# High and low parts of the activations through one 512-column matmul in the feed-forward stages

## The chip, the cores and the metric

The kernel runs on one NeuronCore of a Trainium2 chip. The metric is the device time of one execution in microseconds, lower is better. All inputs and outputs are float32, and there is one launch.

## The reference

Two transformer-like blocks run one after the other on 256 tokens of width 1024. Between them they hold four SwiGLU feed-forward layers of width 2816 and two squared-ReLU MLPs of width 4096. The other stages are a state-space mixer (S5) and three attentions.

```python
def swiglu(h, w_gate, w_up, w_down):
    return (jax.nn.silu(h @ w_gate) * (h @ w_up)) @ w_down

def first_block(x, ...):                       # DEPTH = 2, D_MODEL = 1024, D_FF = 2816
    h = x                                      # (1, 256, 1024) float32
    for layer in range(DEPTH):
        h = h + 0.5 * swiglu(rms_norm(h, ffn_norm[layer, 0]), ...)
        hn = rms_norm(h, mix_norm[layer])
        h = h + (s5_mixer(hn, ...) if layer % 2 == 0 else moba_mixer(hn, ...))
        h = h + 0.5 * swiglu(rms_norm(h, ffn_norm[layer, 1]), ...)
    return h

def second_block(x, ...):                      # D_FF_2 = 4096
    h = x
    for layer in range(DEPTH):
        hn = rms_norm_2(h, norm_mix_g[layer])
        h = h + (ab attention if layer % 2 == 0 else mla attention)
        hn = rms_norm_2(h, norm_mlp_g[layer])
        h = h + jnp.square(jax.nn.relu(hn @ mlp_w1[layer])) @ mlp_w2[layer]
    return rms_norm_2(h, final_norm_g)
```

## The kernel before, in words

Activations lie feature-major: partition = feature within a block of 128, free axis = the 256 tokens (T). There are KT = 8 such blocks of the width 1024. Every projection in float32 is done in three parts. A matrix W is split as whi = W rounded to the matmul's reduced format (fp32r) and wlo = W - whi, the activations likewise into xhi and xlo, and W x is taken as whi xhi + whi xlo + wlo xhi. One call of `mm3` (L551) issues these three matmuls of 256 columns each, in this order, all into the same half of a PSUM bank; each matmul instruction loads its own stationary 128x128 tile, so whi is loaded twice.

The weights of all stages are one stream of 246 chunks of 128x2048 floats (1 MB). For each chunk n SyncE loads `raw` (three slots), ScalarE casts it into `whi` (`split_hi`, L979; it waits until TensorE has used the chunk three before, semaphore `w_used`), VectorE subtracts to get `wlo` (`split_lo`, L1285), and TensorE waits for `wlo_ready` and runs 48 matmuls on it. A chunk of a gate or up matrix gives 2 x 128 output features (16 `mm3`), a chunk of a down matrix takes 2 x 128 hidden features to all 1024 outputs (16 `mm3`).

The stages ffn0, ffn1, ffn2, ffn3 have 11 iterations of three chunks (gate, up, down), the stages mlp0 and mlp1 16 iterations of two (up, down). The first gate and up of a stage are done ahead by `proj_first` and `proj`, then a loop on every engine runs the rest: `ffn` and `mlp` on TensorE issue for iteration i the gate and up of i and then the down of i-1. `down` adds into banks 0 to 3 over the whole stage. Gate and up go to banks 4 to 7, two pairs in turn in `ffn`, three banks in turn in `mlp`, one bank for each chunk.

VectorE's order within an iteration with first chunk c is: `split_lo(c+2)`, `gate`, `split_lo(c+3)`, `hidden`, `split_lo(c+4)`. `gate` (L1322) reads the bank, multiplies by the inverse root `rstd` of the norm and writes `gs`; ScalarE takes the SiLU of it. `hidden` reads the up bank times rstd into `us` (L1331), multiplies by `gs` (L1336, in the MLPs the squared ReLU, L1338), ScalarE casts to `hhi` (L1018), VectorE subtracts to get `hlo` (L1341), and only then comes `split_lo(c+4)`. All waits are semaphores, and each engine runs its list in the written order. GpSimd prepares tables for the S5 stage while ffn0 runs (L448 to L484).

The sums over the 1024 features for the norm go through bank 7 (`stats`), and ScalarE takes the root from there (`root_ready`).

Of the kernel before, what the change touches and what calls it, by code (L numbers as in the profile page):

```python
# [14 lines left out]
ALU = mybir.AluOpType  # L15
# [33 lines left out]


BEFORE = {}
_it = _swiglu = _n = 0
for _name, _ in STAGES:
    if _name[:3] in ("ffn", "mlp"):
        BEFORE[_name] = dict(gs=_swiglu, us=_it, act=_it, hid=_it, hhi=_it, hlo=_it, acc=3 * _n)
        _its = FFN_IT if _name[:3] == "ffn" else MLP_IT
        _it, _swiglu, _n = _it + _its, _swiglu + (_its if _name[:3] == "ffn" else 0), _n + 1
N_NORMS = len(STAGES) + 1


# [11 lines left out]
def build(nc, wstream, xT, params, tgain, s5b, s5c, causal, onehot, logn, relb, out, scratch):  # L72
# [3 lines left out]
    def S(name):  # L76
        if name not in sems:
            sems[name] = ctx.enter_context(nc.semaphore(name))
        return sems[name]
# [11 lines left out]
    with ctx:  # L91
# [2 lines left out]
        wlo = sb("wlo", [P, NSLOT, CH], F32R)  # L94
        h = sb("h", [P, KT, T])
        at[0] += 448
        xhi = sb("xhi", [P, KT, T], F32R)
        xlo = sb("xlo", [P, KT, T], F32R)
        gs = sb("gs", [P, 2, T])
        us = sb("us", [P, 2, T])  # L100
        at[0] += 32
# [103 lines left out]

        def both(v):
            return v.unsqueeze(1).to_broadcast([P, 2, T])

        def half_bank(b, m):
            return ps[:, b, m * T:(m + 1) * T]  # L210
# [99 lines left out]
        def roots_upto(k):  # L310

            return sum(not token_major(n) for n in range(k + 1))
# [234 lines left out]
        def _(pe):  # L547
# [12 lines left out]
            def proj(n, i, bank, operand=None, wait_k=None, first_k=0, stop_k=None):  # L560
# [12 lines left out]
                if stop_k is None:  # L573
                    last.then_inc(S("w_used"), 1)

            def proj_first(n, bank, wait_k, operand=None):

                ohi, olo = operand or (xhi, xlo)
                slot = n % NSLOT
                chunk_ready(n, None)  # L580
                for k in range(KT):
                    pe.wait_ge(*wait_k(k))
                    for m in range(2):
                        w = slice(m * P, (m + 1) * P)
                        last = mm3(half_bank(bank, m), whi_b[slot][:, k, w], wlo_b[slot][:, k, w],
                                   ohi[:, k, :], olo[:, k, :], k == 0 and m == 0, k == KT - 1)
                last.then_inc(S("w_used"), 1)
# [57 lines left out]
            def ffn(st):  # L645
                F, k = FIRST[st], NORM_OF[st]
                proj_first(F, 4, x_wait(k))
                start_stage(k)
                zero_acc()
                proj(F + 1, None, 5)  # L650
                stats(k)
                with pe.Fori(0, (FFN_IT - 1) // 2) as i:
                    for u in range(2):
                        b, n = (1 + u) % 2, F + 2 + 3 * u

                        proj(n, i, 4 + 2 * b)
                        if u == 0:
                            pe.wait_ge(S("root_ready"), roots_upto(k))
                        proj(n + 1, i, 5 + 2 * b)
                        down(st, n + 2, u, i, u)  # L660
                down(st, F + 3 * FFN_IT - 1, FFN_IT - 1, None, (FFN_IT - 1) % 2, final=True)

            def mlp(st):
                F, k = FIRST[st], NORM_OF[st]
                proj_first(F, 4, x_wait(k))
                stats(k)
                start_stage(k)
                zero_acc()
                with pe.Fori(0, (MLP_IT - 1) // 3) as i:
                    for u in range(3):  # L670
                        n = F + 1 + 2 * u
                        proj(n, i, 4 + (1 + u) % 3)
                        down(st, n + 1, u, i, u)
                down(st, F + 2 * MLP_IT - 1, MLP_IT - 1, None, (MLP_IT - 1) % 3, final=True)

# [596 lines left out]
        def _(dve):  # L1272
# [41 lines left out]
                dve.reciprocal(rstd[:, :], rstd[:, :]).then_inc(S("rstd_ready"), 1)  # L1314
                dve.wait_ge(S("rstd_ready"), n)

            def gate(st, i0, i, b, n_gate):

                dve.wait_ge(S("w_used"), at_iter(n_gate + 1, BODY, i))
                if i0 > 0:  # L1320
                    dve.wait_ge(S("hidden_ready"), at_iter(BEFORE[st]["hid"] + i0, 2, i))
                dve.tensor_tensor(gs[:, :, :], bank2(4 + 2 * b), both(rstd[:, :]), ALU.mult)\  # L1322
                    .then_inc(S("gate_scaled"), 1)

            def hidden(st, i0, i, b, per, n_up):

# [1 line left out]
                swiglu = st.startswith("ffn")  # L1328
                if i0 > 0:
                    dve.wait_ge(S("hidden_lo_ready"), at_iter(BEFORE[st]["hlo"] + i0, per, i))  # L1330
                dve.tensor_tensor(us[:, :, :], bank2(5 + 2 * b if swiglu else 4 + b), both(rstd[:, :]), ALU.mult)\  # L1331
                    .then_inc(S("up_scaled"), 1)
                dve.wait_ge(S("up_scaled"), at_iter(BEFORE[st]["us"] + i0 + 1, per, i))
                if swiglu:
                    dve.wait_ge(S("gate_activated"), at_iter(BEFORE[st]["gs"] + i0 + 1, per, i))
# [11 lines left out]
            def ffn(st):  # L1347
                F, k = FIRST[st], NORM_OF[st]
                split_lo(F + 2)
                inverse_root(k)  # L1350
                gate(st, 0, None, 0, F)
                split_lo(F + 3)
                hidden(st, 0, None, 0, 2, F + 1)
                with dve.Fori(0, (FFN_IT - 1) // 2) as i:
                    for u in range(2):
                        c = F + 2 + 3 * u
                        split_lo(c + 2, i)
                        gate(st, 1 + u, i, (1 + u) % 2, c)
                        split_lo(c + 3, i)
                        hidden(st, 1 + u, i, (1 + u) % 2, 2, c + 1)  # L1360
                        split_lo(c + 4, i)
# [377 lines left out]
```

## Time and profile before

| | |
|---|---|
| median of three runs | 1686.85 us (1685.65 to 1688.14) |
| the profiled execution, its own time | 1688.04 us |
| its span, first to last instruction | 1686.2 us |
| TensorE busy with matmuls | 1600.0 us, 95% |
| VectorE busy | 1088.6 us, 65% |
| ScalarE busy | 760.5 us, 45% |
| GpSimd busy | 465.0 us, 28% |
| mean granted TensorE clock | 0.967 of full |

Busy time of TensorE is the time in which any matmul is in flight; one of 256 columns takes 280 ns from start to end, but the next starts after 113 to 118 ns. So the step from start to start, and not the duration, says what a matmul costs in a dense stretch. Starts in the rows are rounded to 10 ns; a step is therefore read over many matmuls.

### The profile page before, as it was taken

The page shows a single profiled execution, that of the slowest core. Times are in us where ns is not written, and L with a number is a line of the kernel's source. Part 1 is how long each engine was busy: PE and PEld are TensorE (multiplying, and loading weights), DVE is VectorE, ACT ScalarE, POOL GpSimd, SP SyncE. Part 2 cuts the span into 40 slices and gives each one's busy share as a digit, 9 for nine tenths or more (in the row PEclk, how much of TensorE's full clock was granted, in tenths as well). Part 3 has the DMA queues.
Part 4 walks back from the last instruction along what each step waited for, and adds up shares of the span by engine and source line. Part 5 has one row for each costly group of instructions (what it writes and reads, how often), then busy time and mean ns, then how long its engine had stood idle before and what let it go on. Part 6 is the DMA issues. An engine that isn't in the chain of part 4 may idle for free.

```text
span 1686.2 us, 31471 instructions
## 1 busy us (share of the span) xinstructions
PE 1600.0 (95%) x13068; PEld 1531.7 (91%) x13068; DVE 1088.6 (65%) x1067; ACT 760.5 (45%) x995; POOL 465.0 (28%) x413
## 2 busy tenths in 40 slices
PE   5989998799999999999999999999999998999997
PEld 5979997599999999999889999976999996699997
DVE  7798769966555665566566555635655665476565
ACT  5434450055344444347554344655434355654432
POOL 6999517700000100007530000564100023510000
PEclk9989996799999999999999999989999997999999
DMA  6535540045555565554425555340555542045552
GB/s 223 196 129 195 211 151 1 1 154 184 187 199 174 173 218 192 181 199 151 150 103 184 197 191 196 136 182 1 182 192 179 194 175 76 25 171 199 179 198 75
DMA packets 39012, 265.74 MB, mean 158 GB/s; under 512 B 4352, under 2 KB 6400, under 8 KB 7328
## 3 DMA queue, kind: packets, MB, share of 16 engines
q1 hardware_dynamic: 37808, 261.41, 44.6%
q0 software_dynamic: 1136, 3.38, 0.8%
q8 instruction: 49, 0.80, 0.2%
q14 instruction: 19, 0.16, 0.0%
HBM read 263.70 MB, written 1.06 MB: 157 GB/s over the span
## 4 chain that ended last, share of the span: by engine, by line
PE 80%; DVE 10%; POOL 4%; issue 3%; ACT 2%; DMA 0%; DVEq 0%; SPq 0%; POOLq 0%; ACTq 0%
PE ps L549 74%; DVE gst L1465 3%; PE ps L839 2%; PE ps L829 2%; DVE wlo L1285 1%; PE ps L817 1%; DVE xlo L1291 1%; POOL tsq L284 1%; DVE h L1301 1%; DVE t L1439 1%; DVE t L1440 1%; ACT pm L1202 0%; DMA h<-in_xT 0%; POOL pm L413 0%; DVE us L1336 0%
## 5 line engine op out<-in xcount | busy, mean ns | idle before, releaser
L1285 DVE TENSOR_TENSOR wlo<-raw,whi 128x2048 fp32r<-128x2048 f32 x246 | 599.0, 2439 | 250.4 <-ACT whi L979 250.1
L549 PE MATMUL ps<-xhi,whi 128*128 128x256 f32 x2048 | 573.5, 280 | 28.9 <-DVE wlo L1285 16.3
L979 ACT CAST whi<-raw 128x2048 fp32r<-128x2048 f32 x246 | 469.2, 1912 | 252.7 <-PE ps L549 252.6
L549 PE MATMUL ps<-xlo,whi 128*128 128x256 f32 x2048 | 570.2, 278 | 0.0
L549 PE MATMUL ps<-xhi,wlo 128*128 128x256 f32 x2048 | 569.6, 278 | 0.0
L549 PEld LDWEIGHTS ps<-xhi,whi 128*128 128x128 f32 x2048 | 388.1, 189 | 33.8 <-DVE wlo L1285 17.4
L549 PEld LDWEIGHTS ps<-xhi,wlo 128*128 128x128 f32 x2048 | 388.5, 190 | 0.0
L549 PEld LDWEIGHTS ps<-xlo,whi 128*128 128x128 f32 x2048 | 387.5, 189 | 0.1
L549 PE MATMUL ps<-hhi,whi 128*128 128x256 f32 x1216 | 341.8, 281 | 0.2
L549 PE MATMUL ps<-hhi,wlo 128*128 128x256 f32 x1216 | 341.6, 281 | 0.0
L549 PE MATMUL ps<-hlo,whi 128*128 128x256 f32 x1216 | 341.3, 281 | 0.0
L359 POOL TENSOR_TENSOR sq<-sq,power 128x256 f32<-128x256 f32 x10 | 16.6, 1658 | 828.7 <-ACT sq L993 828.7
L549 PEld LDWEIGHTS ps<-hhi,whi 128*128 128x128 f32 x1216 | 228.9, 188 | 0.8 <-issue 0.8
L549 PEld LDWEIGHTS ps<-hlo,whi 128*128 128x128 f32 x1216 | 229.1, 188 | 0.0
L549 PEld LDWEIGHTS ps<-hhi,wlo 128*128 128x128 f32 x1216 | 229.0, 188 | 0.0
L1018 ACT CAST hhi<-us 128x512 fp32r<-128x512 f32 x76 | 47.2, 621 | 346.8 <-DVE us L1336 190.9
L549 PE MATMUL ps<-whi,xhi 128*128 128x256 f32 (+1 forms) x368 | 104.7, 285 | 2.6 <-DVE xlo L1291 2.6
L549 PE MATMUL ps<-whi,xlo 128*128 128x256 f32 (+1 forms) x368 | 102.6, 279 | 0.0
L549 PE MATMUL ps<-wlo,xhi 128*128 128x256 f32 (+1 forms) x368 | 102.5, 279 | 0.0
L1331 DVE TENSOR_TENSOR us<-ps,rstd 128x512 f32<-128x512 f32 x76 | 52.5, 690 | 72.1 <-PE ps L549 72.0
L1341 DVE TENSOR_TENSOR hlo<-us,hhi 128x512 fp32r<-128x512 f32 x76 | 59.2, 779 | 52.9 <-ACT hhi L1018 52.9
L549 PE MATMUL ps<-yhi,whi 128*128 128x256 f32 x256 | 73.4, 287 | 1.3 <-DVE ylo L1557 1.3
(235 smaller groups left out, 2071.3 us busy)
## 6 DMA issues: line engine op xcount, KB each, us to landing
raw<-in_wstream SPq DMA_DIRECT2D x247, 1024.0 KB, 4.9
h<-in_xT SPq DMA_DIRECT2D x1, 1024.0 KB, 7.9
out_hT<-h SPq DMA_DIRECT2D x2, 512.0 KB, 3.0
biasA<-bias_rows POOLq DMA_DIRECT2D x5, 192.0 KB, 5.4
biasB<-bias_rows POOLq DMA_DIRECT2D x3, 192.0 KB, 5.5
braw<-in_s5b POOLq DMA_DIRECT2D x1, 512.0 KB, 3.9
CL<-in_s5c POOLq DMA_DIRECT2D x4, 128.0 KB, 5.1
tg<-in_tgain POOLq DMA_DIRECT2D x1, 384.0 KB, 3.5
```

The lines of the kernel that those rows point to most:

```text
L284: chain(eng.tensor_tensor(m1, x1, s, ALU.mult))
L549: return pe.matmul(o, l, r, start=first, stop=last, skip_group_check=True)
L817: last = pe.transpose(ps[:, 2 + s % 2, kt * T + t * P:kt * T + (t + 1) * P], pm[s % 2][:, t, kt * P:(kt + 1) * P], ident)
L829: last = pe.matmul(o, vtok[:, kt, hd["v"]:hd["v"] + hd["dv"]], pT[s % 2][:, kt, q0:T], start=kt == 0, stop=kt == TT - 1, skip_group_check= ...
L839: last = pe.matmul(ps[:, s % 2, t * T:t * T + w], hd["q"][:, t * P:(t + 1) * P], hd["k"][:, 0:w], start=True, stop=True, skip_group_check= ...
L979: act.copy(whi[:, slot, :], raw[:, slot, :]).then_inc(S("whi_ready"), 1)
L1018: act.copy(hid_hi(b), us[:, :, :]).then_inc(S("hidden_hi_ready"), 1)
L1285: dve.tensor_tensor(wlo[:, slot, :], raw[:, slot, :], whi[:, slot, :], ALU.subtract)\
L1291: dve.scalar_tensor_tensor(out=xlo[:, j, :], in0=h[:, j, :], scalar=gain(k, j), in1=xhi[:, j, :], op0=ALU.mult, op1=ALU.subtract).then_inc ...
L1331: dve.tensor_tensor(us[:, :, :], bank2(5 + 2 * b if swiglu else 4 + b), both(rstd[:, :]), ALU.mult)\
L1341: dve.tensor_tensor(hid_lo(b), us[:, :, :], hid_hi(b), ALU.subtract).then_inc(S("hidden_lo_ready"), 1)
L1465: dve.tensor_tensor_scan(gst[g % 2][:, rr, ri, :], m2, t1[g % 2][:, rr, ri, :], 0.0, ALU.mult, ALU.add).then_inc(S("s5_scan"), 1)
```

## The change

xhi and xlo become the two halves of one tensor `xx`. In the loops of the ffn and mlp stages a new `proj_wide` takes the place of `proj`: for each of the 16 pairs of output block and k, one matmul of 512 columns moves xhi and xlo of that k through whi, into the left and right half of a whole bank, and one of 256 columns adds wlo xhi to the left half. A chunk now fills two banks (one for each block of 128 outputs): gate banks 6 and 7, up banks 4 and 5, the same ones in each iteration. `gate` and `hidden` on VectorE first add the two halves with a `reduce_sum` out of PSUM into `gs` or `us`, and then multiply this by rstd in place. The first gate and up of a stage, the down projections and all other stages stay as they were. In the first pass of the ffn loop the second half of the gate waits for `root_ready` and the second half of the up for the first iteration's `up_scaled`. In the mlp loop each up waits for `up_read`, VectorE's read of the one before.

```diff
-        xhi = sb("xhi", [P, KT, T], F32R)
-        xlo = sb("xlo", [P, KT, T], F32R)
+        xx = sb("xx", [P, 2, KT, T], F32R)
+        xhi, xlo = xx[:, 0], xx[:, 1]
...
+        def parts(b):
+            return ps[:, b:b + 2, :].rearrange("p m (a t) -> p m t a", a=2)
...
+            def proj_wide(n, i, bank, before_second=None):
+                slot = n % NSLOT
+                chunk_ready(n, i)
+                for m in range(2):
+                    if m == 1 and before_second:
+                        pe.wait_ge(*before_second)
+                    w = slice(m * P, (m + 1) * P)
+                    for k in range(KT):
+                        mm(ps[:, bank + m, :].rearrange("p (a t) -> p a t", a=2), whi_b[slot][:, k, w], xx[:, :, k, :],
+                           k == 0, False)
+                        last = mm(half_bank(bank + m, 0), wlo_b[slot][:, k, w], xhi[:, k, :], False, k == KT - 1)
+                last.then_inc(S("w_used"), 1)
...
-                        proj(n, i, 4 + 2 * b)
-                        if u == 0:
-                            pe.wait_ge(S("root_ready"), roots_upto(k))
-                        proj(n + 1, i, 5 + 2 * b)
+                        proj_wide(n, i, 6, before_second=(S("root_ready"), roots_upto(k)) if u == 0 else None)
+                        proj_wide(n + 1, i, 4,
+                                  before_second=(S("up_scaled"), BEFORE[st]["us"] + 1) if u == 0 else None)
                         down(st, n + 2, u, i, u)
...
-                        proj(n, i, 4 + (1 + u) % 3)
+                        pe.wait_ge(S("up_read"), at_iter(BEFORE[st]["wide"] + u, 3, i))
+                        proj_wide(n, i, 4)
                         down(st, n + 1, u, i, u)
...
-                dve.tensor_tensor(gs[:, :, :], bank2(4 + 2 * b), both(rstd[:, :]), ALU.mult)\
-                    .then_inc(S("gate_scaled"), 1)
+                    dve.reduce_sum(gs[:, :, :], parts(6), AX.X).then_inc(S("gate_read"), 1)
+                    dve.wait_ge(S("gate_read"), at_iter(BEFORE[st]["wide"] + i0, 2, i))
+                    src = gs[:, :, :]
+                else:
+                    src = bank2(4)
+                dve.tensor_tensor(gs[:, :, :], src, both(rstd[:, :]), ALU.mult).then_inc(S("gate_scaled"), 1)
...
-                dve.tensor_tensor(us[:, :, :], bank2(5 + 2 * b if swiglu else 4 + b), both(rstd[:, :]), ALU.mult)\
-                    .then_inc(S("up_scaled"), 1)
+                    dve.reduce_sum(us[:, :, :], parts(4), AX.X).then_inc(S("up_read"), 1)
+                    dve.wait_ge(S("up_read"), at_iter(BEFORE[st]["wide"] + i0, per, i))
+                    src = us[:, :, :]
+                else:
+                    src = bank2(5 if swiglu else 6)
+                dve.tensor_tensor(us[:, :, :], src, both(rstd[:, :]), ALU.mult).then_inc(S("up_scaled"), 1)
```

TensorE at the start of the ffn0 loop, before: the gate chunk is triples of 256 columns.

```order
L549 MATMUL ps<-xhi,whi 128x256 [waits wlo_ready]
L549 MATMUL ps<-xlo,whi 128x256
L549 MATMUL ps<-xhi,wlo 128x256
L549 MATMUL ps<-xhi,whi 128x256
L549 MATMUL ps<-xlo,whi 128x256
L549 MATMUL ps<-xhi,wlo 128x256
```

The same place now (`xx` is the tensor that holds xhi and xlo):

```order
L555 MATMUL ps<-xx,whi 128x512 [waits wlo_ready]
L555 MATMUL ps<-xx,wlo 128x256
L555 MATMUL ps<-xx,whi 128x512
L555 MATMUL ps<-xx,wlo 128x256
L555 MATMUL ps<-xx,whi 128x512
L555 MATMUL ps<-xx,wlo 128x256
```

Each triple has become a pair with the same number of columns, one instruction and one load of whi fewer.

VectorE in one iteration of the ffn loop, before (`wlo` is `split_lo`, `gs` the gate, `us` the up and hidden values):

```order
L1285 TENSOR_TENSOR wlo<-raw,whi 128x2048
L1319 REGISTER_ALU
L1321 ISA
L1322 TENSOR_TENSOR gs<-ps,rstd 128x512
L1284 REGISTER_ALU
L1285 TENSOR_TENSOR wlo<-raw,whi 128x2048
L1327 REGISTER_ALU
L1331 TENSOR_TENSOR us<-ps,rstd 128x512
L1333 REGISTER_ALU
L1336 TENSOR_TENSOR us<-us,gs 128x512
L1341 TENSOR_TENSOR hlo<-us,hhi 128x512
```

And now:

```order
L1306 TENSOR_TENSOR wlo<-raw,whi 128x2048
L1340 REGISTER_ALU
L1342 ISA
L1343 TENSOR_REDUCE gs<-ps 128x512
L1348 TENSOR_TENSOR gs<-gs,rstd 128x512
L1305 REGISTER_ALU
L1306 TENSOR_TENSOR wlo<-raw,whi 128x2048
L1352 REGISTER_ALU
L1356 TENSOR_REDUCE us<-ps 128x512
L1361 TENSOR_TENSOR us<-us,rstd 128x512
L1362 REGISTER_ALU
L1365 TENSOR_TENSOR us<-us,gs 128x512
```

A reduction that reads 1024 values in each partition stands ahead of each multiplication by rstd, which now has both operands in SBUF; everything behind it on VectorE, the next `wlo` first, comes later by that.

## Rows read from the trace of the kernel before

**Rows 1.** Page, part 1: busy time and instructions of each engine.

```profile
PE 1600.0 (95%) x13068; PEld 1531.7 (91%) x13068; DVE 1088.6 (65%) x1067; ACT 760.5 (45%) x995; POOL 465.0 (28%) x413
```

**Rows 2.** Chain that ended last, 400 to 570 us: start, length, what.

```profile
407.26 157.06 PE ps L549 x1356
```

**Rows 3.** Groups by form, TensorE: busy us, mean ns; idle before, releaser.

```profile
L549 PE MATMUL ps<-xhi,whi 128*128 128x256 f32 x2048 | 573.5, 280 | 28.9 <-DVE wlo L1285 16.3 <-DVE xlo L1291 12.6
```

**Rows 4.** Windows: length, busy of PE, PEld, DVE, ACT, POOL, clock, DMA.

```profile
81.00:98.00 17.00, 17.00 (x149) 17.00 (x149) 16.17 (x8) 6.90 (x5) 16.68 (x5) 1.00 0.40 131
98.00:116.00 18.00, 10.26 (x89) 10.06 (x87) 17.28 (x5) 6.02 (x4) 17.69 (x5) 0.84 0.30 110
171.00:188.00 17.00, 17.00 (x150) 17.00 (x149) 14.79 (x8) 7.02 (x6) 16.52 (x7) 1.00 0.57 192
430.00:556.00 126.00, 126.00 (x1097) 126.00 (x1096) 73.52 (x53) 51.88 (x38) 0.00 (x0) 1.00 0.56 191
```

**Rows 5.** Timeline of TensorE, an ffn1 projection: first and last of 43 matmuls.

```profile
431.08 0.28 PE L549 MATMUL ps<-xhi,whi 128*128 128x256 f32 x1
...
435.84 0.28 PE L549 MATMUL ps<-xhi,whi 128*128 128x256 f32 x1
```

**Rows 6.** The same, an ffn0 down projection: first and last of 23.

```profile
126.78 0.28 PE L549 MATMUL ps<-hhi,whi 128*128 128x256 f32 x1
...
129.38 0.28 PE L549 MATMUL ps<-hlo,whi 128*128 128x256 f32 x1
```

**Rows 7.** The same, mla stage, 384 columns: first and last of 9.

```profile
1409.06 0.34 PE L549 MATMUL ps<-whi,cqhi 128*128 128x384 f32 x1
...
1410.46 0.34 PE L549 MATMUL ps<-whi,cqlo 128*128 128x384 f32 x1
```

**Rows 8.** The same, 512 columns: first and last of five, twice.

```profile
1413.83 0.40 PE L549 MATMUL ps<-wlo,ckhi 128*128 128x512 f32 x1
...
1414.77 0.39 PE L549 MATMUL ps<-whi,cklo 128*128 128x512 f32 x1
...
1416.10 0.39 PE L549 MATMUL ps<-wlo,ckhi 128*128 128x512 f32 x1
...
1417.03 0.40 PE L549 MATMUL ps<-whi,cklo 128*128 128x512 f32 x1
```

**Rows 9.** Groups by form, VectorE, as Rows 3.

```profile
L1549 DVE TENSOR_REDUCE mx<-ps 128x2 f32<-128x512 f32 x24 | 16.6, 691 | 31.1 <-PE ps L839 31.1
L1547 DVE TENSOR_REDUCE mx<-lg 128x1 f32<-128x128 f32 x8 | 2.3, 287 | 0.3
```

**Rows 10.** Timeline of VectorE in ffn0, 96 to 117 us.

```profile
96.76 5.13 DVE L1285 TENSOR_TENSOR wlo<-raw,whi 128x2048 fp32r<-128x2048 f32 x1
101.81 0.68 DVE L1331 TENSOR_TENSOR us<-ps,rstd 128x512 f32<-128x512 f32 x1
102.53 4.32 DVE L1336 TENSOR_TENSOR us<-us,gs 128x512 f32<-128x512 f32 x1
```

**Rows 11.** Timeline of GpSimd there.

```profile
99.82 6.48 POOL L450 TENSOR_TENSOR Ec<-Ec,etmp 128x2016 f32<-128x2016 f32 x1
106.37 3.97 POOL L451 TENSOR_TENSOR Es<-Es,Ec 128x2016 f32<-128x2016 f32 x1
```

**Rows 12.** Timeline of TensorE there.

```profile
116.58 0.58 PE L549 MATMUL ps<-xhi,whi 128*128 128x256 f32 x1 [8.32 <-DVE wlo L1285]
```

**Rows 13.** Timeline of VectorE, start and first pass of the ffn1 loop.

```profile
400.93 0.68 DVE L1331 TENSOR_TENSOR us<-ps,rstd 128x512 f32<-128x512 f32 x1
...
407.05 0.68 DVE L1322 TENSOR_TENSOR gs<-ps,rstd 128x512 f32<-128x512 f32 x1
409.84 0.69 DVE L1331 TENSOR_TENSOR us<-ps,rstd 128x512 f32<-128x512 f32 x1
410.56 0.69 DVE L1336 TENSOR_TENSOR us<-us,gs 128x512 f32<-128x512 f32 x1
413.75 2.29 DVE L1285 TENSOR_TENSOR wlo<-raw,whi 128x2048 fp32r<-128x2048 f32 x1 [1.12 <-ACT whi L979]
```

More of the change, by code:

```diff
@@ L51 @@
 BEFORE = {}
-_it = _swiglu = _n = 0
+_it = _swiglu = _n = _wide = 0
 for _name, _ in STAGES:
     if _name[:3] in ("ffn", "mlp"):
-        BEFORE[_name] = dict(gs=_swiglu, us=_it, act=_it, hid=_it, hhi=_it, hlo=_it, acc=3 * _n)
+        BEFORE[_name] = dict(gs=_swiglu, us=_it, act=_it, hid=_it, hhi=_it, hlo=_it, acc=3 * _n,
+                             wide=_wide)
         _its = FFN_IT if _name[:3] == "ffn" else MLP_IT
         _it, _swiglu, _n = _it + _its, _swiglu + (_its if _name[:3] == "ffn" else 0), _n + 1
+        _wide += _its - 1
 N_NORMS = len(STAGES) + 1
@@ L653, in ffn @@
                     for u in range(2):
-                        b, n = (1 + u) % 2, F + 2 + 3 * u
-                        proj(n, i, 4 + 2 * b)
-                        if u == 0:
-                            pe.wait_ge(S("root_ready"), roots_upto(k))
-                        proj(n + 1, i, 5 + 2 * b)
+                        n = F + 2 + 3 * u
+                        proj_wide(n, i, 6, before_second=(S("root_ready"), roots_upto(k)) if u == 0 else None)
+                        proj_wide(n + 1, i, 4,
+                                  before_second=(S("up_scaled"), BEFORE[st]["us"] + 1) if u == 0 else None)
                         down(st, n + 2, u, i, u)
@@ L664, in mlp @@
                 F, k = FIRST[st], NORM_OF[st]
-                proj_first(F, 4, x_wait(k))
+                proj_first(F, 6, x_wait(k))
                 stats(k)
@@ L1315, in inverse_root, with gate @@
                 dve.wait_ge(S("rstd_ready"), n)
-            def gate(st, i0, i, b, n_gate):
+            def gate(st, i0, i, n_gate):
                 dve.wait_ge(S("w_used"), at_iter(n_gate + 1, BODY, i))
@@ L1350, in ffn @@
                 inverse_root(k)
-                gate(st, 0, None, 0, F)
+                gate(st, 0, None, F)
                 split_lo(F + 3)
@@ L1357, in ffn @@
                         split_lo(c + 2, i)
-                        gate(st, 1 + u, i, (1 + u) % 2, c)
+                        gate(st, 1 + u, i, c)
                         split_lo(c + 3, i)
```

## The prediction

> **What bounds the kernel now.** I read part 1 of the page first: TensorE has a matmul in flight for 1600 of 1686 us, and its weight loads are busy for 91% [rows 1]. The chain of waits says the same by stage. In ffn1 it is one unbroken piece of 157 us of TensorE from the first down to the end of the stage [rows 2], and the window inside it shows TensorE busy for 126 of 126 us at the full clock (1.00, that is 2.4 GHz) with VectorE at 73.5 of 126, 58% [rows 4]. The same holds for the other ffn and mlp stages. So in those loops two things count: the step from one matmul's start to the next, and whether VectorE's `wlo` keeps coming in time.
>
> The exception is ffn0. GpSimd prepares the S5 tables then. From 98 to 116 us VectorE is busy for 17.28 and GpSimd for 17.69 of 18 us, while TensorE falls to 10.26 and its clock to 0.84 [rows 4], and one wait of 8.32 us for `wlo` ends that stretch [rows 12]. That single wait is half of all that the projections waited for `wlo` (16.3 us) [rows 3]. The reason stands in the timelines. The subtraction that takes 2.29 us when GpSimd is idle [rows 13] takes 5.13 us here; the multiplication us<-us,gs, 0.69 us alone [rows 13], takes 4.32 us; and it ends at 106.85, about 0.5 us after GpSimd's 128x2016 operation ends at 106.30 [rows 10, 11]. GpSimd's operations take 3.97 us, or 6.48 us when VectorE's work falls into them [rows 11]. These two take turns whenever VectorE's operands all lie in SBUF. The multiplications that read PSUM kept their 0.68 us in the very same stretch [rows 10].
>
> **What the change removes on TensorE.** The loops hold 4 x 10 x 2 = 80 gate and up chunks and 2 x 15 = 30 up chunks of the MLPs, 110 in all, with 16 pairs each: 1760 places where two matmuls of 256 columns (and two loads of the same whi) become one of 512. The number of columns stays, so what can be saved is only what a matmul costs beyond its columns.
>
> Now the steps. In an ffn1 projection, 42 steps take 4.76 us, 113.3 ns each [rows 5]; the columns alone are 256 / 2.4 GHz = 106.7 ns, so 6.6 ns lie on top. In a down projection 22 steps take 2.60 us, 118.2 ns [rows 6]. If those 6.6 ns were a fixed price of an instruction, longer matmuls would show them once. They don't. With 384 columns, 8 steps take 1.40 us, 175 ns [rows 7], 15 ns over the 160 of the columns. With 512, 4 steps take 0.94 and 0.93 us, 235 and 232.5 ns [rows 8], 19 to 22 ns over 213.3. The excess grows with the columns: per column 0.443 and 0.462 ns at 256, 0.456 at 384, 0.454 to 0.459 at 512. A matmul of 512 costs as much as two of 256, within the spread of the two kinds of 256.
>
> Two of 256 in these loops are 226.7 ns. For the new one I take 230 ns, between 226.7 and the 232.5 of rows 8, since its moving operand is the one that went at the lower step. That is +3.3 ns x 1760 = +6 us. Bounds from the rows: the bare columns, 213.3 ns, give -13.4 x 1760 = -24 us; the slowest rows, 235 ns for the wide one and 118.2 instead of 113.3 for the narrow one behind it, give (8.3 + 4.9) x 1760 = +23 us.
>
> The Trainium skill, page TensorE: Matmul & The Clock Gate, section Back-to-back issue gap, gives the step as N/2.4 + 2.5 ns, so 216 ns for 512 columns. By it the wide one would save 11 ns a time, about 19 us, and the sum below would be near 1681. The trace does not agree with it at 512 columns of this type (232.5 to 235 ns), so I leave it to a rival.
>
> **What the change adds on VectorE.** Each of the 110 reads gets a reduction over 1024 values in a partition. Reductions of 128 and 512 values take 287 and 691 ns [rows 9], 1.05 ns for each further value, so 1024 take 691 + 539 = 1.23 us. The multiplication behind it now reads SBUF instead of PSUM: 0.69 us without GpSimd, as the 0.69 of PSUM [rows 13]. With the semaphore between them a read costs 1.27 us more.
>
> In ffn1 to ffn3 and both MLPs this is hidden. An ffn iteration is three chunks, 16.6 us, in which VectorE has some 7 us free by the 58%; two conversions take 2.5. The tightest place is the first pass of a loop. TensorE starts the first down at 407.26 [rows 2]; 96 matmuls later, at 118.2 ns, that is at 418.6, it wants the `wlo` that VectorE makes from 413.75 to 416.04 [rows 13]. Both conversions (at 407.05 and 409.84) stand ahead of it, also by way of ScalarE's casts, so it comes at 416.04 + 2.54 = 418.6. It just fits; I take 0, with 1.5 us in all as the upper end. The new waits there are met early: the second half of the loop's first up starts 24 matmuls (2.8 us) before 407.26, at 404.4, and the up before it was read at 400.93 [rows 13], a read that the change leaves as it is. The `up_read` wait of an mlp stage has a whole down projection (48 x 118.2 ns = 5.7 us) to be met in.
>
> In ffn0 nothing hides it. Between 81 us and the end of the long wait at 116.58 VectorE is full (16.17 of 17 and 17.28 of 18 us [rows 4]) and three conversions stand in its list (the us of the iteration before at the start of the stretch, the gs just ahead of the wlo of 96.76, the us of 101.81 [rows 10]). The least that each costs is 1.27 us, 3.8 in all. The most: the multiplication, now with both operands in SBUF, takes a turn behind one more GpSimd operation of 3.97 us [rows 11], so 1.23 + 3.97 = 5.2 each, 15.6 in all. I take 3 each, since GpSimd's list is finite and a turn taken earlier is missing later: +9 us on the one long wait. In the four iterations after it VectorE is busy for 14.79 of 17 us [rows 4]. 2.2 us are free and two conversions with two short waits for GpSimd (0.6 each, a guess between 0 and a turn) want 3.7, so 1.5 x 4 = 6 us at most, 0 at least; I take 3. Together +12 us for ffn0, from 3.8 to 21.6.
>
> **Sum.** 6 + 12 + 0 = +18 us. The profiled execution took 1688.04 us (span 1686.2), so 1706; it lies 1.2 us above the median of the runs, and on the median's scale the forecast is 1686.85 + 18, about 1704 us.
>
> **The rivals.** A: the wide matmul goes near the clock, because the excess at 256 belongs to the loads, and half of those for whi are gone. For it: weight loads are busy as much as the array [rows 1]. Against it: in rows 7 and 8 each load has 384 or 512 columns to hide behind, and the excess is larger. At 213.3 to 220 ns a time it saves 12 to 24 us; with +12 from ffn0 the time is 1675 to 1687. It is faster by a measurable amount when the step is under about 217 ns.
>
> B, the slow side of my own case: ffn0 alone as forecast by the upper ends (+21.6) and the slow matmul rows (+10 to +23): 1718 to 1731. It decides once `wlo` is late in ffn0 behind the long wait too: TensorE then shows waits in every iteration until GpSimd's list is done. The window from 171 us speaks for it (GpSimd still busy for 16.52 of 17 us), and against it that TensorE waited nowhere there [rows 4].
>
> C: the reduction takes the values of a partition in pairs that lie 256 floats apart in PSUM, which no row shows. If that doubled the reading, 1.07 us more for each conversion, the first pass of the three tight loops would wait 2.1 us each (6 us) and ffn0 gains 3 x 1.07 + 4 x 2.1 = 12 us of VectorE work: about 1722. The Trainium skill, Advanced Engine Details and Errata, section PSUM Cachelines, says that every two consecutive elements should be contiguous for best throughput; it speaks of matmuls, and no run here shows it for VectorE.
>
> D: the two ends cancel, a step of 220 to 224 ns (-5 to -12 us) against ffn0 at its lower half: 1684 to 1690, no change.
>
> **Chances.** My forecast 0.5 (1693 to 1716), A 0.2, B 0.12, C 0.08, D 0.1. A change of less than 0.2%, 3.4 us, can't be told from none. Faster: most of A, 0.19. Same: D's middle and the rim of A, 0.08. Slower: 0.73. The range takes in half of A and most of B and C: 1681 to 1722. The likeliest case's own range is 1693 to 1716.
>
> **What the profile after would show.** In the loops of ffn1 a wide matmul and a narrow one together step at about 343 ns against 340 before; under 333 is A, over 350 B. The stretch of TensorE in ffn1 would be 157 to 159 us. The reduction would be 1.23 us; 2 us or more is C. The long wait of TensorE for `wlo` in ffn0 would be about 17 us instead of 8.3, and us<-us,rstd there would take more than 0.69. The forecast is wrong if the step of the wide matmul is that of its columns, or if ffn0's wait stays at 8 us.

## The result and the profile after

The kernel became slower. Its median is 1727.45 us (1725.56 to 1730.66, four runs) against 1687.49 us for the kernel before in the same comparison, a ratio of 1.0242 with a 95% interval of 1.022 to 1.0264. The profiled execution took 1728.38 us, 40.3 us more than the 1688.04 of before. The forecast was 1704 with a range of 1681 to 1722: the direction was right and the time lies outside.

I cut both traces at the zeroing of banks 0 to 3 (the start of a stage's loops) and at the last down matmul of the stage:

```
stage, zeroing to last down, us    before   after   difference
ffn0                               199.4    222.7   +23.3
ffn1, ffn2, ffn3 (each)            179.5    182.8    +3.3
mlp0, mlp1 (each)                  173.8    176.7    +2.9
all six                           1085.5   1124.5   +39.0   (of 40.3)
```

The times run from the start of the zeroing to the start of the last down matmul. So there are two costs: about 3 us in every stage (19 us in the six), and some 20 us more in ffn0 alone. In the page, part 1 answers to [rows 1]:

```profile
PE 1625.5 (94%) x11308; PEld 1471.5 (85%) x11308; DVE 1228.9 (71%) x1177; ACT 762.9 (44%) x995; POOL 456.9 (26%) x413
```

1760 matmuls and loads are gone (13068 to 11308), and the time that loads take fell by 60 us. TensorE still has a matmul in flight for 25 us more. What its projections wait for stands in the groups of the page, in the line that answers to [rows 3]:

```profile
L555 PE MATMUL ps<-xx,whi 128*128 128x512 f32 (+1 forms) x2336 | 739.0, 373 | 43.1 <-DVE wlo L1306 29.9
```

They waited 29.9 us for `wlo`, where it was 16.3. The windows (length, then busy time of TensorE, its loads, VectorE, ScalarE, GpSimd, then the clock and the DMA) answer to [rows 4]; the last one is 126 us inside ffn1:

```profile
81.00:98.00 17.00, 16.76 (x106) 14.99 (x104) 16.75 (x7) 0.75 (x2) 16.69 (x5) 0.94 0.48 176
98.00:116.00 18.00, 7.58 (x29) 6.53 (x30) 17.43 (x5) 5.90 (x4) 17.76 (x4) 0.62 0.22 65
171.00:188.00 17.00, 16.18 (x99) 14.77 (x100) 15.53 (x9) 2.97 (x4) 14.47 (x6) 0.90 0.51 185
450.00:576.00 126.00, 126.00 (x836) 115.19 (x836) 89.50 (x68) 52.57 (x38) 0.00 (x0) 1.00 0.50 183
```

In ffn1 TensorE has no gap at the full clock, before and after, so its 3.3 us are longer steps and no wait. In ffn0 all three windows show TensorE short of its time; the one from 171 us, which was full before, now has 16.18 of 17 us. The granted clock in the three is 0.94, 0.62 and 0.90, where it was 1.00, 0.84 and 1.00.

The step in an ffn1 projection, from TensorE's timeline (start, length, what), first and last of 15 wide matmuls, with the narrow one behind the first:

```profile
476.75 0.40 PE L555 MATMUL ps<-xx,whi 128*128 128x512 f32 x1
476.98 0.28 PE L555 MATMUL ps<-xx,wlo 128*128 128x256 f32 x1
...
481.69 0.40 PE L555 MATMUL ps<-xx,whi 128*128 128x512 f32 x1
```

14 pairs take 4.94 us, 353 ns each. At the finer starts that the trace holds, the wide matmul takes 235.0 ns and the narrow one 118.3. Three times the 113.3 of [rows 5] is 340.

VectorE's timeline in ffn0, 82 to 119 us, answers to [rows 10]:

```profile
84.09 1.22 DVE L1348 TENSOR_TENSOR gs<-gs,rstd 128x512 f32<-128x512 f32 x1
85.23 4.53 DVE L1306 TENSOR_TENSOR wlo<-raw,whi 128x2048 fp32r<-128x2048 f32 x1
89.68 1.21 DVE L1356 TENSOR_REDUCE us<-ps 128x512 f32<-128x1024 f32 x1
90.92 2.88 DVE L1361 TENSOR_TENSOR us<-us,rstd 128x512 f32<-128x512 f32 x1
93.84 4.01 DVE L1365 TENSOR_TENSOR us<-us,gs 128x512 f32<-128x512 f32 x1
98.54 4.20 DVE L1370 TENSOR_TENSOR hlo<-us,hhi 128x512 fp32r<-128x512 f32 x1 [0.69 <-ACT hhi L1039]
...
115.18 3.76 DVE L1348 TENSOR_TENSOR gs<-gs,rstd 128x512 f32<-128x512 f32 x1
```

The reductions keep their 1.21 us beside GpSimd. The multiplications by rstd, which took 0.68 us out of PSUM, take 1.22, 2.88 and 3.76. The `wlo` behind all this comes so late that TensorE stands still (the wait in brackets, with what ended it):

```profile
78.99 0.50 PE L555 MATMUL ps<-xx,whi 128*128 128x512 f32 x1 [2.82 <-DVE wlo L1306]
108.42 0.79 PE L555 MATMUL ps<-xx,whi 128*128 128x512 f32 x1 [10.66 <-DVE wlo L1306]
```

Waits of 3.1, 2.3 and 2.5 us follow; they end at 131, 152 and 172 us. Before, the long wait was the only one after the start of the stage [rows 12]. At the start both kernels wait 7.7 to 7.9 us; that wait ends at 34 us. The waits of ffn0 in one line each (TensorE's line, what it waited for: us in all, times, longest), before and after:

```profile
PE ps L549 <- DVE wlo L1285: 16.0, 2, 8.3
PE ps L555 <- DVE wlo L1306: 29.6, 7, 10.7
```

So TensorE waits 13.6 us more in ffn0. The steps at the full clock give 3.3 us, as in the other ffn stages. Of the 23.3 us, 6.4 are left. Most of them lie in matmuls at the half clock behind the waits. The window behind the long wait, and the first and last wide matmul of six pairs in it:

```profile
108.40:113.70 5.30, 5.28 (x17) 4.51 (x18) 5.30 (x1) 0.00 (x0) 5.22 (x2) 0.50 0.60 198
```

```profile
109.22 0.63 PE L555 MATMUL ps<-xx,whi 128*128 128x512 f32 x1
...
113.06 0.63 PE L555 MATMUL ps<-xx,whi 128*128 128x512 f32 x1
```

Six pairs take 3.84 us, 640 ns each instead of 353. The granted clock was 0.50 behind four of the five waits from 76 us on, for 3.0 to 5.3 us each time (15 us together), and 1.00 behind the one that ends at 152 us. Before there was one such stretch there, 3.8 us long, behind the long wait. From these lengths and steps I estimate 5 of the 6.4 us.

### The profile page after: what moved, and what is told of

Same layout as the page of the kernel before. It is cut to its first block, busy times and chain, and to the rows that moved or that the text cites. A ratio compares the mean times of both kernels' runs of the same rounds, so it can differ in the third digit from the quotient of the medians.

```text
span 1726.6 us, 28146 instructions
## 1 busy us (share of the span) xinstructions
PE 1625.5 (94%) x11308; PEld 1471.5 (85%) x11308; DVE 1228.9 (71%) x1177; ACT 762.9 (44%) x995; POOL 456.9 (26%) x413
## 4 chain that ended last, share of the span: by engine, by line
PE 73%; DVE 15%; issue 4%; POOL 4%; ACT 3%; DMA 0%; DVEq 0%; ACTq 0%; SPq 0%; POOLq 0%
PE ps L555 67%; DVE wlo L1306 4%; DVE gst L1494 2%; PE ps L860 2%; PE ps L850 2%; ACT whi L1000 1%; DVE xx L1312 1%; PE ps L838 1%; POOL tsq L290 1%; DVE us L1365 1%; DVE us L1361 1%; DVE h L1322 1%; DVE us L1356 1%; DVE t L1468 1%; DVE t L1469 1%
## 5 line engine op out<-in xcount | busy, mean ns | idle before, releaser
L555 PE MATMUL ps<-xx,whi 128*128 128x512 f32 (+1 forms) x2336 | 739.0, 373 | 43.1 <-DVE wlo L1306 29.9
L555 PE MATMUL ps<-xx,wlo 128*128 128x256 f32 x2048 | 579.1, 283 | 0.0
L555 PEld LDWEIGHTS ps<-xx,whi 128*128 128x128 f32 x2336 | 424.3, 191 | 129.5 <-DVE wlo L1306 32.7
L555 PEld LDWEIGHTS ps<-xx,wlo 128*128 128x128 f32 x2048 | 389.8, 190 | 0.1
L555 PE MATMUL ps<-whi,xx 128*128 128x256 f32 (+1 forms) x736 | 136.0, 282 | 2.8 <-DVE xx L1312 2.5
L1356 DVE TENSOR_REDUCE us<-ps 128x512 f32<-128x1024 f32 x70 | 85.6, 1222 | 74.1 <-PE ps L555 74.1
L555 PEld LDWEIGHTS ps<-whi,xx 128*128 128x128 f32 x736 | 114.1, 188 | 5.4 <-DVE xx L1312 3.7
L555 PE MATMUL ps<-wlo,xx 128*128 128x256 f32 (+1 forms) x368 | 102.7, 279 | 0.0
L1343 DVE TENSOR_REDUCE gs<-ps 128x512 f32<-128x1024 f32 x40 | 48.9, 1221 | 38.1 <-PE ps L555 38.1
L555 PE MATMUL ps<-ylo,whi 128*128 128x256 f32 x256 | 72.4, 283 | 0.0
```

The source lines that it names most:

```text
L555: return pe.matmul(o, l, r, start=first, stop=last, skip_group_check=True)
L1343: dve.reduce_sum(gs[:, :, :], parts(6), AX.X).then_inc(S("gate_read"), 1)
L1356: dve.reduce_sum(us[:, :, :], parts(4), AX.X).then_inc(S("up_read"), 1)
```

## The experiments

Kernels compared in one table of stages first (us, zeroing to last down, from the profiled execution; ratio against before with its 95% interval):

```
run                      median    ratio                     ffn0   ffn1  mlp0
e1  halves apart         1712.08   1.0144 [1.0127, 1.0161]   221.6  179.4 173.8
e2  no reduction         1713.18   1.016  [1.0141, 1.0178]   201.6  182.8 181.0
e3  multiply from PSUM   1721.29   1.0198 [1.0181, 1.0215]   202.0  182.8 181.0
e5  e3, wait mended      1715.64   1.0169 [1.0152, 1.0186]   207.2  182.9 176.7
e6  e2, wait mended      1703.74   1.0102 [1.008, 1.0124]    201.0  182.8 176.7
e8  before, SBUF operand 1706.27   1.0108 [1.0088, 1.0127]   219.5  179.5 173.8
e9  SiLU to PSUM         1682.51   0.9975 [0.9963, 0.9987]   193.6  179.5 173.8
e10 hidden in PSUM       1678.55   0.9938 [0.9922, 0.9955]   189.2  179.5 173.8
e11 hidden 32 B lower    1675.67   0.9928 [0.9912, 0.9945]   200.9  182.4 169.6
e13 e10 and e11          1667.70   0.9882 [0.9839, 0.9924]   191.5  182.4 169.6
```

**The 512 columns or something beside them.** The first run takes the wide matmul apart and leaves all else of the change.

```diff
-    mm(whole_bank, whi_b[slot][:, k, w], xx[:, :, k, :], k == 0, False)
+    mm(half_bank(bank + m, 0), whi_b[slot][:, k, w], xhi[:, k, :], k == 0, False)
+    mm(half_bank(bank + m, 1), whi_b[slot][:, k, w], xlo[:, k, :], False, False)
```

> The changed kernel with each 512-column matmul issued as two of 256 (whi xhi to the left half, whi xlo to the right half, then wlo xhi to the left); banks, waits and VectorE's work as changed. The changed kernel steps in pairs of 235 + 118 = 353 ns against 340 ns before, 13.3 ns x 1760 = up to 23 us of the 40 lost. Theory 'length': the 512-column matmul itself costs this; then triples take 340 ns again and the time is 1728 - 20 = about 1708 us. Rival 'layout': it is the second half bank and the order of the outputs that break the 113.3 ns step; then the triple stays at 3 x 118 = 354 ns and the time at about 1727 us.

Measured: 1712.08 us, and ffn1 to ffn3 and the MLPs are back at 179.3 to 179.4 and 173.8 us. In this timeline `x2` is a row of two matmuls; nine triples lie between the two rows:

```profile
459.75 0.39 PE L555 MATMUL ps<-xx,whi 128*128 128x256 f32 x2
...
462.81 0.39 PE L555 MATMUL ps<-xx,whi 128*128 128x256 f32 x2
```

That is 3.06 us, 340 ns a triple. The same columns into the same banks cost 13 ns more when two matmuls are made one. All that is left of the loss (24 us) is ffn0, 22.2 us over before.

**Which form of 512 columns.** The next kernel was executed once. Each of its stages issues the projections in its own form: ffn0 as changed, ffn1 halves apart, ffn2 the two of the left half first, ffn3 the wide one alone with wlo xhi left out, mlp0 512 contiguous columns (so the values are other ones), mlp1 eight wide ones and then eight narrow ones.

```diff
+FORM = dict(ffn0="wide", ffn1="split", ffn2="grouped", ffn3="wide_only", mlp0="contiguous", mlp1="phases")
```

> Read for the steps alone, stage by stage; parts of the sums are left out or wrong in four stages. ffn0 as changed; ffn1 split as in e1 (left, right, left); ffn2 with the two left matmuls together (left, left, right); ffn3 512-column matmuls alone, without wlo xhi; mlp0 the 512 columns contiguous in SBUF; mlp1 eight of 512 and then eight of 256 for each block. Theory 'rate': a 512-column fp32r matmul costs 235 ns wherever it stands (0.459 ns a column), so 235 alone, contiguous and in phases. Rival 'mixture': the alternation of 512 and 256 upsets an even step; then ffn3 and the first half of mlp1 step at 216 to 227 ns. Rival 'two pieces': the jump from xhi to xlo costs it; then mlp0 alone steps at 216 to 227. For ffn1 and ffn2: 113.3 each by 'length', 118 where the second half bank upsets it.

Measured: 114.4 to 114.9 ns with halves apart in either order; the wide one 233 ns alone, 234.9 with contiguous columns, 233.6 in a row of eight. Neither the mixture with narrow ones nor the two pieces of the moving operand is the cause. A matmul of 512 columns of this type takes 233 to 235 ns.

**What VectorE's part costs.** The next runs take out the reductions, or only the SBUF operand of the multiplication; in both the right halves don't get into the result. The edit in `gate` (that in `hidden` alike), e3 first and then e2:

```diff
     dve.reduce_sum(gs[:, :, :], parts(6), AX.X).then_inc(S("gate_read"), 1)
-    src = gs[:, :, :]
+    src = ps[:, 6:8, 0:T]
```

```diff
-    dve.reduce_sum(gs[:, :, :], parts(6), AX.X).then_inc(S("gate_read"), 1)
-    src = gs[:, :, :]
+    src = ps[:, 6:8, 0:T]
```

> The changed kernel without the reductions: VectorE multiplies the left halves by rstd straight out of PSUM, so the right halves (whi xlo) are left out of the result. TensorE's list is as changed. Theory: VectorE's added work costs only in ffn0, about 19 us there; so ffn0 goes back to one wait of about 8 us and the time to about 1708 us, with the steps of 353 ns kept. Rival: the reductions also cost in the other stages; then more than 22 us come back.

> The changed kernel with the reductions kept, but the multiplication by rstd behind each reads the left halves in PSUM and not the reduced sum in SBUF, so the right halves are left out of the result. It tells the two parts of VectorE's added work apart. Theory 'turns': most of the 19 us in ffn0 is the multiplication with both operands in SBUF, which waits for GpSimd; then some 10 to 13 us come back, 1715 to 1718 us. Rival 'length': the 1.22 us of each reduction are the price; then at most 4 us come back, 1724 us or more.

Both had ffn0 at about 202 us in the profiled execution, but mlp0 and mlp1 went up from 176.7 to 181.0: the wait that I had put in place of `up_read` counted the first up of a stage too and held TensorE at each start. So these times are not to be used, and the two were repeated with a counter of their own (e5 and e6).

> As e3_multiply_from_psum (reductions kept, the multiplication by rstd reads the left halves in PSUM, the right halves are left out of the result), but TensorE's wait in the mlp stages counts loop passes alone: in e2 and e3 my own wait for the first up held each mlp stage for 4.3 us, 8.6 us in all. Theory 'turns': ffn0 as in e3 (202 us from its zeroing to its last down, against 222.7 as changed and 199.4 before) and a time of 1715.2 - 8.6 = 1706.6 us. If the runs without a profile stay near 1713 as those of e3 stood at 1721, something in them goes another way than in the profiled one.

> As e2_no_reduce (no reductions, multiplication from PSUM, right halves left out), with the same mend of the wait. What is left of the change is TensorE's list. Theory: only the steps remain, 1760 pairs at 353 ns for 340, less where the triples before did not run at 340 either: 1713.2 - 8.6 = 1704.6 us. Rival: single banks for gate and up cost something besides; then 1708 or more.

Measured: without reductions 1703.74 us and ffn0 at 201.0. What is left, about 16 us, is TensorE's steps: the five other stages have 15.7 us more than before, and ffn0 has 1.6, with 1.2 us less of waits than before. With the reductions and a multiplication out of PSUM 1715.64 us, ffn0 at 207.2: the reductions cost up to 6 us there. The 1706.6 us expected of e5 were missed, since its ffn0 didn't come out like that of e3. How much the reductions cost is not sharp: e3, with the same operations, had ffn0 at 202.0 in a profiled execution of 1715.16 us, 6 us under its own median, and of the 11.9 us between the medians of e5 and e6 some 4 to 5 lie, in the profiled executions, in stages that the edit doesn't touch. From e5 to the changed kernel there are 15.5 us more in ffn0 and 11.8 between the medians, and these are the place of one operand. The line of e5's waits:

```profile
PE ps L555 <- DVE wlo L1306: 19.5, 5, 8.7
```

**The operand alone, in the kernel before.** Here TensorE and the number of values read stay as before; only a copy to SBUF is put ahead of each multiplication by rstd.

```diff
+    dve.tensor_copy(gs[:, :, :], src).then_inc(S("gate_read"), 1)
+    src = gs[:, :, :]
     dve.tensor_tensor(gs[:, :, :], src, both(rstd[:, :]), ALU.mult)
```

> The kernel before with VectorE's part of the change alone: in the loops each gate and up is copied from PSUM to SBUF (512 values, about 0.69 us instead of the reduction's 1.22) and multiplied by rstd in SBUF. TensorE's list is that of before. Theory 'turns': ffn0 grows by about 18 to 21 us as it did in the changed kernel, although each read is only 0.7 us longer without GpSimd, and the other stages by nothing: 1706 to 1709 us. Rival 'length': 0.7 us for each of some 10 reads while VectorE is full, +7 us, 1695 us.

Measured: 1706.27 us; ffn0 took 20.1 us more and every other stage the same as before. VectorE's timeline there:

```profile
116.28 0.68 DVE L1343 COPY us<-ps 128x512 f32<-128x512 f32 x1
116.99 4.30 DVE L1346 TENSOR_TENSOR us<-us,rstd 128x512 f32<-128x512 f32 x1
```

The copy out of PSUM keeps its 0.68 us, the multiplication takes 4.30. This is the same loss as in the change, without a wide matmul and without a reduction. The Trainium skill, page SBUF — State Buffer, section SBUF: two separate sides, says that a VectorE operation with two SBUF inputs and a GpSimd operation that reads SBUF take one pair of ports in turn, each for its whole length. The trace agrees: the multiplication of 4.30 us ends at 121.29, about 0.5 us after GpSimd's operation that ends at 120.74.

**The other way round: operands out of SBUF.** If that is so, the kernel before can gain. ScalarE writes the SiLU into the gate's bank (e9), and VectorE also writes the hidden values into the up's bank (e10).

```diff
-    act.activation(gs[:, :, :], gs[:, :, :], ACT.Silu)
+    act.activation(bank2(4 + 2 * (i0 % 2)), gs[:, :, :], ACT.Silu)
-    dve.tensor_tensor(us[:, :, :], us[:, :, :], gs[:, :, :], ALU.mult)
+    dve.tensor_tensor(us[:, :, :], us[:, :, :], bank2(4 + 2 * b), ALU.mult)              # e9
+    dve.tensor_tensor(bank2(5 + 2 * b), us[:, :, :], bank2(4 + 2 * b), ALU.mult)         # e10
+    act.copy(hid_hi(b), bank2(5 + 2 * b))                                                # e10
+    dve.tensor_tensor(hid_lo(b), bank2(5 + 2 * b), hid_hi(b), ALU.subtract)              # e10
```

> The kernel before, with one thing changed in the feed-forward stages: ScalarE writes the SiLU of the gate into the gate's own bank of PSUM instead of back into gs, so that VectorE's us<-us,gs reads one operand from PSUM. Theory of turns: only an operation of VectorE with all operands in SBUF waits for GpSimd. Then this multiplication takes 0.7 us in ffn0 too instead of up to 4.3 us, TensorE's one wait for wlo in ffn0 (8.6 us) shrinks by 1 to 4 us, and the time is 1684 to 1687. Rival: one operand in SBUF is enough to wait for GpSimd (the multiplications out of PSUM so far had rstd, a small vector read twice, as the other); then it still takes up to 4.3 us and the time stays at 1688. Everything outside ffn0 stays as it is in both.

> As the run before, and VectorE also writes the hidden values into the up's bank of PSUM, from where ScalarE casts them to hhi and VectorE takes them for hlo. By the theory of turns the last two operations of an iteration with all operands in SBUF, apart from wlo, are gone: us<-us,gs and hlo take 0.7 us each in ffn0, TensorE's wait in ffn0 shrinks from 8.6 us by 4 to all of it, and the time is 1680 to 1684. Rival: a turn not taken at these two is taken at the next wlo, whose length grows by as much; then ffn0 stays at 199 us and the time at 1688.

Measured: 1682.51 and 1678.55 us. VectorE's groups in ffn0 (30 to 218 us), first of before, then of e10:

```profile
L1285 DVE TENSOR_TENSOR wlo<-raw,whi 128x2048 fp32r<-128x2048 f32 x33 | 107.8, 3281 | 15.1 <-ACT whi L979 15.0
L1336 DVE TENSOR_TENSOR us<-us,gs 128x512 f32<-128x512 f32 x11 | 15.4, 1403 | 0.4
L1341 DVE TENSOR_TENSOR hlo<-us,hhi 128x512 fp32r<-128x512 f32 x11 | 14.2, 1288 | 7.6 <-ACT hhi L1018 7.6
```

```profile
L1285 DVE TENSOR_TENSOR wlo<-raw,whi 128x2048 fp32r<-128x2048 f32 x34 | 101.3, 2986 | 28.5 <-ACT whi L979 28.5
L1336 DVE TENSOR_TENSOR ps<-us,ps 128x512 f32<-128x512 f32 x11 | 7.7, 696 | 0.4
L1341 DVE TENSOR_TENSOR hlo<-ps,hhi 128x512 fp32r<-128x512 f32 x11 | 7.6, 692 | 7.2 <-ACT hhi L1018 7.2
```

One operand in PSUM is enough: 1403 ns become 696 and 1288 become 692, and the turns are not made up for at `wlo`, as the rival had it. ffn0 falls from 199.4 to 189.2 us, and the stretch that was the worst of the kernel [rows 4] is full of matmuls at the full clock:

```profile
98.00:116.00 18.00, 18.00 (x159) 18.00 (x158) 16.19 (x8) 6.83 (x5) 17.77 (x4) 1.00 0.51 175
```

The clock there was 0.84 before and is 1.00 now, so with the wait its slow stretch is gone too. Both kernels gained more in ffn0 than their waits shrank: e9 5.8 us for 4.3 us less of waits, e10 10.2 for 8.1. Both times lie a little under what I expected (1684 to 1687 and 1680 to 1684).

**Why 113 here and 118 there.** The step of 256 columns had two values [rows 5, 6], and the change moved its narrow matmuls from one to the other. First, in the kernel before, other orders of the down matmuls, one for each stage:

```diff
+DOWN = dict(ffn0="asis", ffn1="f_outer", ffn2="grouped", ffn3="f_outer_grouped", mlp0="banks", mlp1="phases")
```

> The kernel before with other orders of the down matmuls, read for the steps by stage: ffn0 as it was; ffn1 all blocks of f=0, then of f=1; ffn2 within a triple whi hhi, wlo hhi, whi hlo; ffn3 both; mlp0 the outputs ordered so that a block's neighbour in its bank comes four later; mlp1 all whi hhi, then all whi hlo, then all wlo hhi. Down steps are 118.3 ns before, the projections' 113.3. Theory 'change of operand': what is read or written anew every three or six matmuls breaks the even step; then one of ffn1, ffn3, mlp1 comes to 113 to 114. Rival 'place': it is the place of hhi and hlo in SBUF; then all stay at 118. At 113.3 everywhere the kernel before would gain 5 ns x 3648 = 18 us.

Measured: 118.2 to 118.4 ns in the mean of each, 1687.16 us in one execution. Order, bank and change of operand have no part in it. Then the place of the operands in SBUF (x starts 64 bytes over a multiple of 128, the hidden values 96 over one; the edit moves what lies behind the hidden values too):

```diff
-        at[0] += 32
         hid_at = at[0]
```

> The kernel before with hhi and hlo (and all that lies behind them in SBUF) 32 bytes lower. The x operands start at 64 bytes over a multiple of 128, the hidden ones at 96 over one; here both start at 64. Theory that the place of the moving operand sets the step: the down matmuls go from 118.3 to 113.3 ns, 76 chunks x 48 x 5.0 ns = 18 us less, 1670. Rival, the place has no part in it: 118.3 stays, and the time is 1688.

Measured: 1675.67 us, and two steps in one execution. The profiled execution (1691.47, the highest of five; the others took 1672.5 to 1678.3) has 118 ns for projections and downs alike in all ffn stages, and 113 for both in the MLPs. TensorE's timeline, 12 steps in ffn1, then 41 steps in mlp0:

```profile
459.96 0.28 PE L548 MATMUL ps<-hhi,whi 128*128 128x256 f32 x1
...
461.37 0.28 PE L548 MATMUL ps<-hhi,whi 128*128 128x256 f32 x1
...
1251.13 0.28 PE L548 MATMUL ps<-hlo,whi 128*128 128x256 f32 x1
...
1255.77 0.28 PE L548 MATMUL ps<-hhi,whi 128*128 128x256 f32 x1
```

1.41 us over 12 are 117.5 ns, 4.64 us over 41 are 113.2. So 113 is no property of the x operand. With both operands at 64 bytes the step is kept from a projection into a down and for whole stages; in the kernel before and e7, with different places, the downs always fell to 118. My expectation (all downs at 113, -18 us) held for the MLPs alone. What decides which of the two a stage falls into was not found.

With the hidden values in PSUM as well:

> The kernel before with the edits of e10 (SiLU and hidden values in PSUM in the feed-forward stages) and of e11 (hidden operands 32 bytes lower) together. If they are independent, -9 us from ffn0 and -10 us from TensorE's steps add up to 1668 to 1670. Rival: the step of 113 or 118 ns that a stage falls into changes from build to build, and then anything from 1664 to 1683 is possible, with single runs far apart as in e11 (1672 to 1691).

Measured: 1667.70 us (1661.92 to 1676.68), the fastest of all, 1.2% under before. The two gains add up, though single executions lie nearly as far apart as in e11. The chain of waits of its profiled execution shows ffn1 and ffn3, the same 1356 matmuls, where [rows 2] has 157.06:

```profile
399.07 159.98 PE ps L548 x1356
...
897.95 153.98 PE ps L548 x1356
```

**A place at which the wide matmul is free.** The changed kernel with x at 32, 0 and 96 bytes over a multiple of 128, for example:

```diff
-        at[0] += 448
+        at[0] += 416
         xx = sb("xx", [P, 2, KT, T], F32R)
```

> The changed kernel with xhi and xlo 32 bytes lower, at 32 bytes over a multiple of 128 (all else where it was), for the steps alone. If the place of the moving operand sets the step, that of the wide and of the narrow matmul (235 and 118 ns) moves by several ns, up or down, a pair of 353 to 340 or less being a version of the change that costs nothing on TensorE. If 512 columns of this type take 235 ns wherever they lie, the pair stays at 353 and the time at 1728.

> The changed kernel with xhi and xlo at 0 bytes over a multiple of 128, hidden operands where they were. If the excess of a matmul depends on where its moving operand starts, the pair leaves 353 ns (64 bytes) and 347 (32 bytes); at 340 or less the change would be free on TensorE and the time would be 1712 as in the run with the halves apart (e1). If only 32 bytes was special, it is 353 and 1728 again.

> As the run before, with xhi and xlo at 96 bytes over a multiple of 128, the same class as the hidden operands. Here the step may also stay what it is from one operand to the next, so that downs go at another step than 118.3 too. Pair 340 or less: free. Pair 347 to 353: 512 columns in one matmul of this type cost more wherever they lie.

Measured, means in ffn1 (wide + narrow): 230 + 118 = 347 ns at 32 bytes, 231 + 121 = 352 at 0, 235 + 119 = 354 at 96 (230 + 118 in ffn2 of the same execution; the downs were at 118 there, though x and the hidden values share that place). The times are 1722.75 (one execution), 1727.39 (ratio 1.0233, 1.021 to 1.0256) and 1726.54 us (1.0228, 1.0208 to 1.0248). TensorE's timeline at 32 bytes, four pairs in 1.39 us:

```profile
476.78 0.39 PE L555 MATMUL ps<-xx,whi 128*128 128x512 f32 x1
...
478.17 0.39 PE L555 MATMUL ps<-xx,whi 128*128 128x512 f32 x1
```

The place moves the pair by some ns, and none of the four reaches the 340 of three separate matmuls.

## Why the prediction was wrong

**What bounds the kernel.** Right: steps of TensorE in five stages, VectorE and GpSimd in ffn0. Outside the six stages 1.3 of the 40.3 us were lost.

**The matmul term, forecast +6 us, measured +16 (e6) to +19 (the six stages together).** This is the first step that failed, by its size, and the largest part of the miss. I took 230 ns for the wide one, "since its moving operand is the one that went at the lower step", and left the narrow one at 113.3. Measured are 235.0 and 118.3, that is the upper end of my own bounds for both. The reason that I gave was wrong: e11 shows that the low step does not belong to the operand. 13.3 ns x 1760 would be 23 us. It was less because the triples of before did not all go at 340: some chunks at the start of the loops in ffn1 to ffn3 went at the slower step, and the mean over a stage was 342 to 344.

**ffn0 on VectorE, forecast +12 us, measured +20 to +22** (e8 20.1; e1, without wide matmuls, 22.2). The mechanism was right, VectorE's turns with GpSimd. The step that failed is that the sum holds waits alone: it has no term for the clock. I had read the 0.84 beside the wait [rows 4] and gave it no price. In the changed kernel the matmuls at the half clock behind the waits are most of 6.4 us; in e8 waits are 12.2 us more than before and 7.9 us lie beside them.

The waits themselves came to +13.6 us against the 12 of the sum, and that is luck in part, since the terms were off both ways. The long wait grew by 2.4 us, from 8.3 to 10.7, and not by 9; it came one iteration earlier (after the third down of the stage and not the fourth), with a new one of 2.8 us before it. Behind it I took 3 us, the half of an upper end of 6, and 8.0 came. The guess of 0.6 us for a short wait was not the fault: from 119 to 190 us the seven multiplications by rstd took 0.69 to 1.68 us, 1.38 in the mean, that is 0.7 over their length alone. Why 8.0 us came for 3 is not shown. My reading is that I counted VectorE's free 2.2 us [rows 4] as if they could be used to the end, although the turns with GpSimd come in pieces. The reductions, 1.22 us each, have the small part: e1 has ffn0 2.1 us over e8, which has a copy of 0.68 in their place.

**The other stages at 0.** Right. The pass that "just fits" does: ffn1 has no gap, and the new waits are met.

**Rivals.** What happened is nearest to B; I had given it 0.12 and a time of 1718 to 1731. What it was to show came: waits in several iterations of ffn0, and a pair over 350 ns. But its +21.6 us for ffn0 were waits alone, 15.6 of them in the long one; 13.6 us of waits came and the rest was the half clock, so the fit of its time is in part luck. A is refuted: 233 ns even with the wide matmul alone. The Trainium skill, page TensorE: Matmul & The Clock Gate, section Back-to-back issue gap, gives N/2.4 + 2.5 ns, 216 ns at 512 columns, as the gap of an isolated matmul, a condition that my prediction left out; for a stream of loads and matmuls it gives about 131 ns. The trace agrees with neither for this type at 512 columns in any place or form that was run, 230 to 235 ns. C is refuted by 1.22 us for the reduction, against 1.23 forecast from [rows 9]. D needed a step of 220 to 224.

## What to carry to other kernels

Making two matmuls one saves nothing where the step grows with the columns: read the step at the new size from the trace, and where the rows give two values take the upper one, unless something shows why the lower should hold. While GpSimd works, keep one operand of each VectorE operation in PSUM if it can be; here that was worth 9 us in the kernel before (e10) and 12 in the changed one (e5), and the operation's own length without GpSimd (0.69 us both ways) doesn't tell it. Where a wait of TensorE is forecast, look at the granted clock behind such a wait in the trace and price the matmuls there as well: here that was another 6 to 8 us on 12 to 14 us of waits.

## What the runs showed of the hardware

- 256 columns in fp32r had two steady steps in the kernel before and its variants, 113.3 and 117.5 to 118.3 ns, at the full clock and with the same instructions; behind a wide matmul it was 117.6 to 119, and 120 to 121 with x at 0 bytes over a multiple of 128. Only with x and the hidden values both at 64 bytes over a multiple of 128 did whole stages, downs too, go at 113, and not each one did. What decides it is open.
- 512 columns of the same type take 230 to 235 ns in the mean of an undisturbed stage, by place and by stage, 16 to 22 ns over their 213.3.
- A VectorE operation with both tensors in SBUF took up to 4.3 us beside GpSimd instead of 0.69; with one of them in PSUM, as input, 0.69 each time. A reduction of 1024 values in pairs 256 apart in PSUM took 1.22 us, GpSimd busy or not.
- In ffn0 of the changed kernel the granted clock fell to 0.50 by four of five waits for `wlo` (2.5 to 10.7 us) and stayed there for 3.0 to 5.3 us of matmuls, in which a pair took 640 ns instead of 353. It stayed at 1.00 behind a wait of 2.3 us, and in e9 behind one of 2.9 us.
